# Feed-forward of a decoder layer in FP32 on TensorE: Strassen block products for two of eight K pairs, hidden rows turned through DRAM

## What is computed

```python
x = layer_norm(DEEPNORM_ALPHA * x + merged @ w_out[l], ln_g[l, 0], ln_b[l, 0])
ffn = (jax.nn.silu(x @ w_gate[l]) * (x @ w_up[l])) @ w_down[l]
x = layer_norm(DEEPNORM_ALPHA * x + ffn, ln_g[l, 1], ln_b[l, 1])
```

## Time and profile before

| | us |
|---|---|
| three runs | 1892.26, 1892.47, 1892.53 |
| median | 1892.47 |
| span of the profiled execution | 1889.9 |

### The profile page before, as it was taken

The page is one execution under the profiler, slowest core; times in us unless marked ns, Lnnn a source line. Parts: engine busy times, 40 slices in busy tenths (PEclk is TensorE's granted clock), DMA queues, the critical chain, the costliest instruction groups (busy, mean ns, idle before and its releaser), DMA issues.

```text
span 1889.9 us, 29981 instructions
## 1 busy us (share of the span) xinstructions
PE 1876.0 (99%) x9647; PEld 1548.7 (82%) x9647; DVE 1322.6 (70%) x1859; ACT 919.6 (49%) x1234; POOL 184.7 (10%) x448
## 2 busy tenths in 40 slices
PE   9999999999999999999999999999999999999997
PEld 7888888878888888888888887888888888888886
DVE  7878888888676767675677657577775466654656
ACT  5656565664455555556444447444443444443442
POOL 0202020020023233333000000000000000000000
PEclk9999999999999999999999999999999999999999
DMA  7667666575567776776665775566666666665565
GB/s 276 220 202 223 204 214 225 188 242 166 189 198 240 219 245 214 241 222 209 203 193 195 233 237 169 199 189 195 193 196 194 191 192 197 191 196 192 190 192 175
DMA packets 121041, 389.69 MB, mean 206 GB/s; under 512 B 14512, under 2 KB 27632, under 8 KB 120816
## 3 DMA queue, kind: packets, MB, share of 16 engines
q1 hardware_dynamic: 97904, 351.65, 58.2%
q10 hardware_dynamic: 19200, 28.34, 4.9%
q0 software_dynamic: 3840, 8.39, 1.6%
HBM read 368.91 MB, written 19.42 MB: 205 GB/s over the span
## 4 chain that ended last, share of the span: by engine, by line
PE 97%; DVE 1%; DMA 0%; issue 0%; ACT 0%; SPq 0%; DVEq 0%; ACTq 0%
PE pg L496 92%; PE B L496 5%; DVE gates L1474 1%; DMA raw<-in_weights 0%; PE B L596 0%; ACT whi L870 0%; PE B L816 0%; DVE wlo L1466 0%; DVE act_b L1466 0%; PE B L744 0%; DVE lnst L2170 0%; DVE sm L1474 0%; DVE act_a L1466 0%; DVE lnst L2175 0%; ACT L1390 0%
## 5 line engine op out<-in xcount | busy, mean ns | idle before, releaser
L1466 DVE TENSOR_TENSOR wlo<-raw,whi 128x1024 fp32r<-128x1024 f32 (+1 forms) x640 | 778.6, 1219 | 472.8 <-ACT whi L870 454.2
L870 ACT ACTIVATE whi<-raw 128x1024 fp32r<-128x1024 f32 (+1 forms) x640 | 674.3, 1057 | 751.8 <-PE pg L496 706.2
L496 PE MATMUL pg<-whi,act_x 128*128 128x512 f32 x2960 | 936.2, 393 | 1.0 <-ACT whi L870 1.0
L496 PEld LDWEIGHTS pg<-whi,act_x 128*128 128x128 f32 x2960 | 555.6, 188 | 120.2 <-issue 3.7
L496 PE MATMUL pg<-wlo,act_x 128*128 128x512 f32 x1480 | 574.7, 390 | 0.0
L496 PE MATMUL pg<-whi,act_a 128*128 128x512 f32 x1632 | 504.7, 389 | 0.1
L496 PEld LDWEIGHTS pg<-whi,act_a 128*128 128x128 f32 x1632 | 306.3, 188 | 64.2 <-DVE act_a L1466 0.8
L496 PEld LDWEIGHTS pg<-wlo,act_x 128*128 128x128 f32 x1480 | 278.1, 188 | 54.9
L496 PE MATMUL pg<-wlo,act_a 128*128 128x512 f32 x816 | 317.5, 389 | 0.0
L496 PEld LDWEIGHTS pg<-wlo,act_a 128*128 128x128 f32 x816 | 153.2, 188 | 31.7
L496 PE MATMUL pg<-whi,act_b 128*128 128x512 f32 x512 | 158.4, 389 | 0.0
(11 more groups left out here) (264 smaller groups left out, 1067.8 us busy)
## 6 DMA issues: line engine op xcount, KB each, us to landing
raw<-in_weights SPq DMA_DIRECT2D x646, 512.0 KB, 4.3
turn_c<-hraw ACTq DMA_DIRECT2D x8, 512.0 KB, 3.3
qT<-turn_c ACTq DMA_DIRECT2D x32, 128.0 KB, 4.5
turn_q<-hraw ACTq DMA_DIRECT2D x6, 512.0 KB, 4.5
gates<-turn_q ACTq DMA_DIRECT2D x24, 128.0 KB, 4.6
turn_p<-gates POOLq DMA_DIRECT2D x12, 192.0 KB, 3.4
gates<-turn_p POOLq DMA_DIRECT2D x48, 48.0 KB, 4.0
decm<-sums_out ACTq DMA_DIRECT2D x4, 512.0 KB, 3.9
```

The costliest lines, as they stand in the source:

```text
L496: return nc.tensor.matmul(o, l, r, start=start, stop=stop)
L870: return nc.scalar.activation(o, i, ACT.Copy, scale=scale)
L1466: return V.tensor_tensor(o, a, b, op)
```

## The change

Groups f = 1 to 10 take gate and up tiles in turn: tile 2p is rows of K pair p of the gate, tile 2p + 1 the same rows of the up matrix. For p in SPOS = (2, 5) the two tiles are one Strassen product (its form with seven products): two halves of the tokens by two K chunks by gate and up. The sums of weight blocks (v13, v24) are made by VectorE from raw and split into hi and lo like any weight (h13, l13, h24, l24); the sums of x are made once, at the end of group 0 (xs). The even tile then has four block products (12 TensorE products), the odd one three (9). They go into four banks of their own besides the four of gate and up rows, which they share partly; VectorE combines them at step 13 (shared_out), after tile 14 (gate_out) and at step 0 of the next group (up_out), and q1 is copied by ScalarE at step 12. silu now runs after gate_out, and the product with it at step 3 of the next group. pg and B take turns as the groups' own banks.

The product is written in another order of columns, goes to DRAM at step 5 and comes back at step 8 in four reads, and one transpose of 128x1024 at step 11 turns it; hi follows at step 12, lo at step 14. The gain goes to steps 5 and 10. All loops of the part are written out, and semaphores of the prologue are merged (not shown; its order of work is the same). The weights lie in memory as before; SyncE loads them in the new order.

```diff
-GAIN = (11, 13)
+GAIN = (5, 10)
+SPOS = (2, 5)
+NS = len(SPOS)
+H_AT, H_AWAY, H_BACK, H_TURN, H_HI, H_LO = 3, 5, 8, 11, 12, 14
...
+        def banks(f):
+            own, other = ([B[0:2], B[2:4]], pg[0] + pg[1])
+            if f in (2, 4, 5, 7, 10):
+                own, other = pg, B
+            return own, other
+        def down_bank(piece, i):
+            if piece == 0:
+                return B[2 * (i % 2):2 * (i % 2) + 2]
+            if piece == 1:
+                return pg[i % 2]
+            return [B[2:4], pg[1], pg[0], pg[1]][i]
+        def is_mixed(s):
+            return 0 <= s < 2 * TPG and s // 2 in SPOS
...
+            def later_in(n, s, at):
+                r = s % RING
+                sp.wait_ge(hi_done, n + s - RING + 1)
+                sp.wait_ge(lo_done, n + s - RING + 1)
+                sp.dma_start(raw[:, r].rearrange("p k n -> p (k n)"), weights[at]).then_inc(raw_full[r], 16)
+            def up(f):
+                for s in range(2 * TPG if f else 0):
+                    later_in(up_at(f), s, up_at(f) + s % 2 * TPG + s // 2)
+            def down(piece, n, f):
...
+            def product(bank, xh, xl, wh, wl, start, stop):
+                mm(bank[:, :], xh, wh, start, False)
+                mm(bank[:, :], xh, wl, False, False)
+                return mm(bank[:, :], xl, wh, False, stop)
+            def plain_tile(m, x, k0, own, first, last):
+                r = m % RING
+                pe.wait_ge(hi_done, m + 1)
+                pe.wait_ge(lo_done, m + 1)
+                for k in range(TK):
+                    for t in range(TOK):
+                        a = slice(t * P, (t + 1) * P)
+                        end = product(own[t], x[:, 0, k0 + k, a], x[:, 1, k0 + k, a], whi[:, r, k, :], wlo[:, r, k, :],
+                                      first and k == 0, last and k == TK - 1)
+                end.then_inc(tile_used, 1)
+            def mixed_tile(f, n, s):
+                own, other = banks(f)
+                v, i, k, m = mixed(f), SPOS.index(s // 2), s // 2 * TK, n + s
+                r, first, last = m % RING, i == 0, i == NS - 1
+                t0, t1 = slice(0, P), slice(P, SEQ)
+                pe.wait_ge(hi_done, m + 1)
+                pe.wait_ge(lo_done, m + 1)
+                if s % 2 == 0:
+                    product(other[0], act_a[:, 0, k, t0], act_a[:, 1, k, t0], whi[:, r, 0], wlo[:, r, 0], first, last)
+                    product(own[0][0], act_a[:, 0, k + 1, t0], act_a[:, 1, k + 1, t0], whi[:, r, 1], wlo[:, r, 1], False, False)
+                    product(other[3], xs[:, i, 2, 0], xs[:, i, 2, 1], v["h13"][:, 0], v["l13"][:, 0], first, last)
+                    end = product(other[2], xs[:, i, 1, 0], xs[:, i, 1, 1], v["h13"][:, 1], v["l13"][:, 1], first, last)
+                else:
+                    product(own[1][0], xs[:, i, 3, 0], xs[:, i, 3, 1], whi[:, r, 1], wlo[:, r, 1], False, False)
+                    product(other[1], xs[:, i, 0, 0], xs[:, i, 0, 1], v["h24"][:, 0], v["l24"][:, 0], first, last)
+                    end = product(own[0][1], act_a[:, 0, k + 1, t1], act_a[:, 1, k + 1, t1], v["h24"][:, 1], v["l24"][:, 1],
+                                  False, False)
+                end.then_inc(tile_used, 1)
...
+            def shared_ready(f):
+                if f in (1, 5, 9):
+                    for e in range(2):
+                        pe.wait_ge(evac[e], E0 + 1 + f // 4 * 2)
+                else:
+                    pe.wait_ge(gate_free, f - 1)
+                    pe.wait_ge(up_free, f - 1)
+                pe.wait_ge(xs_lo, 1)
...
+                tiles, buf = (TPG, TPG, LAST)[piece], (act_x, act_b, act_x)[piece]
+                pe.wait_ge(N["dve_mT"], 1 + NB + f)
                 for i in range(4):
-                    pe.wait_ge(evac[i % 2], g + i // 2)
+                    down_ready(piece, i)
+                    at = down_bank(piece, i)
...
+            def mixed_item(f, n, s):
+                m, v, i = n + s, mixed(f), nth(f, s)
+                r = m % RING
+                act.wait_ge(raw_full[r], 16 * (m // RING + 1))
+                act.wait_ge(tile_used, m - AHEAD)
+                if s % 2 == 0:
+                    copy(whi[:, r], raw[:, r]).then_inc(s_hi, 1)
+                    act.wait_ge(v_sum, 3 * i + 1)
+                    copy(v["h13"], v["v13"]).then_inc(hi_done, 1)
+                else:
+                    copy(whi[:, r, 1], raw[:, r, 1]).then_inc(s_hi, 1)
+                    act.wait_ge(v_sum, 3 * i + 3)
+                    copy(v["h24"], v["v24"]).then_inc(hi_done, 1)
+            def turn_h(f, s):
+                if s == H_AWAY:
+                    act.wait_ge(N["dve_m"], 1 + NB + f + 1)
+                    rows_away(flat(hraw[:, :, :]), turn_q, q_kept)
+                if s == H_BACK:
+                    act.wait_ge(q_kept, 16 * (HEADS_TURNED + f + 1))
+                    blocks_back(turn_q, landed(hraw), q_full)
+                if s == H_HI:
+                    act.wait_ge(N["dve_turn"], 1 + NB + f)
+                    copy(hi(*hidden(f), 4), turned).then_inc(N["act_mT"], 2)
+            def up(f):
+                n = up_at(f)
+                for s in range(0 if f else TPG - 1, 2 * TPG):
+                    if f and is_mixed(s + AHEAD):
+                        mixed_item(f, n, s + AHEAD)
+                    elif f or s > TPG:
                         split(n, s)
+                    if f not in (0, 5, 9):
+                        turn_h(f - 1, s)
+                    if f and s == S_END:
+                        act.wait_ge(tile_used, n + S_END)
+                        copy(mixed(f)["q1"], banks(f)[1][0][:, :]).then_inc(q1_done, 1)
+                    if f and s == 2 * TPG - 1:
+                        act.wait_ge(gate_free, f)
+                        nc.scalar.activation(vda[:, :, :], vda[:, :, :], ACT.Silu).then_inc(silu_done, 1)
...
+            def mixed_item(f, n, s):
+                m, v, i = n + s, mixed(f), nth(f, s)
+                r = m % RING
+                if s % 2 == 0:
+                    for e in range(2):
+                        dve.wait_ge(raw_full[r + e], 16 * (m // RING + 1))
+                    tt(v["v13"], raw[:, r:r + 2, 0], raw[:, r + 1, 0:2], ALU.add).then_inc(v_sum, 1)
+                    dve.wait_ge(s_hi, 2 * i + 1)
+                    dve.wait_ge(tile_used, m - AHEAD)
+                    tt(wlo[:, r], raw[:, r], whi[:, r], ALU.subtract)
+                    dve.wait_ge(v_sum, 3 * i + 1)
+                    tt(v["v24"][:, 0], v["v13"][:, 0], raw[:, r + 1, 1], ALU.add).then_inc(v_sum, 1)
+                    dve.wait_ge(v_sum, 3 * i + 2)
+                    tt(v["v24"][:, 1], v["v24"][:, 0], raw[:, r, 1], ALU.add).then_inc(v_sum, 1)
+                    dve.wait_ge(hi_done, m + 1)
+                    tt(v["l13"], v["v13"], v["h13"], ALU.subtract).then_inc(lo_done, 1)
+                else:
+                    dve.wait_ge(s_hi, 2 * i + 2)
+                    dve.wait_ge(tile_used, m - AHEAD)
+                    tt(wlo[:, r, 1], raw[:, r, 1], whi[:, r, 1], ALU.subtract)
+                    dve.wait_ge(hi_done, m + 1)
+                    tt(v["l24"], v["v24"], v["h24"], ALU.subtract).then_inc(lo_done, 1)
+            def shared_out(f):
+                v, other = mixed(f), [b[:, :] for b in banks(f)[1]]
+                dve.wait_ge(q1_done, f)
+                lnc(tt(v["w"][:, 0], v["q1"], other[1], ALU.add))
+                lnc(tt(v["u3"], v["w"][:, 0], other[2], ALU.add))
+                tt(v["w"][:, 0], other[3], v["w"][:, 0], ALU.subtract)
+                tt(v["w"][:, 1], other[3], v["u3"], ALU.subtract).then_inc(shared_free, 1)
+            def gate_out(f):
+                v, own = mixed(f), banks(f)[0]
+                dve.wait_ge(tile_used, up_at(f) + 2 * TPG - 1)
+                tt(vda[:, 0], own[0][0][:, :], v["q1"], ALU.add)
+                tt(vda[:, 1], own[0][1][:, :], v["u3"], ALU.add).then_inc(gate_free, 1)
+            def up_out(f):
+                v, own = mixed(f), banks(f)[0]
+                dve.wait_ge(tile_used, up_at(f) + 2 * TPG)
+                dve.wait_ge(shared_free, f)
+                for t in range(TOK):
+                    last = tt(v["w"][:, t], v["w"][:, t], own[1][t][:, :], ALU.add)
+                last.then_inc(up_free, 1)
+            by_channel = flat(hraw[:, :, :]).rearrange("p (b h t i) -> p t h b i", b=4, h=HB, t=TOK)
+            def by_head(ap):
+                return ap.rearrange("p (h b i) -> p h b i", h=HB, b=4)
+            def product(f):
+                dve.wait_ge(silu_done, f)
+                dve.wait_ge(up_free, f)
+                w = mixed(f)["w"]
+                if f == FG - 1:
+                    tt(hraw[:, :, :], w, vda[:, :, :], ALU.mult).then_inc(N["dve_m"], 1)
+                    return
+                for t in range(TOK):
+                    last = tt(by_channel[:, t], by_head(w[:, t]), by_head(vda[:, t]), ALU.mult)
+                last.then_inc(N["dve_m"], 1)
```

(108 more changed lines are left out.)

232 lines of the change are left out of this document (126 added, 106 removed).

## The result

The changed kernel takes 1895.17 us (median of 19 runs from 1890.7 to 1900.9; one more run, of 3817.8 us, is left out), the kernel before 1892.26 us (20 runs, 1891.2 to 1894.1). The ratio is 1.0016, interval 1.0009 to 1.0023: **slower by 3 us** where 5.6 us faster was forecast. The 60 products are gone and give 13.6 us, so something new costs 16.5 us. The profiled execution, one of the shorter ones, took 1892.59 us with a span of 1890.4.

What follows compares the result with a forecast made beforehand. TensorE's number of products was taken to bound the kernel. Saving 13.6 us and adding 8.0 us of waits gave -5.6 us, so 1886.9 us from the median 1892.47; range 1879 to 1899.

Steps and rivals of the forecast that it cites:

- 60 products, 13.6 us, in full unless TensorE waits: Two mixed pairs in each of ten groups save 60 TensorE products of 0.2267 us, 13.6 us off the end.
- Spacings 1.14, 0.605, 0.72, a sum of 38.3: VectorE's instructions overlap, so its queue in f = 2 to 4 sums to 38.3 us against TensorE's 42.16.
- The slower rival: Long mixed VectorE instructions don't overlap, so VectorE's queue is the bound: 19.4 us of waits, 1898.3 us; chance 0.22.
- 2.1 us behind silu, margin 0.5 at the first mixed tile, waits at f = 2, 3, 4, 7, 8: VectorE waits 2.1 us at group end, has 0.5 us margin, enters late: 5.8 us of TensorE waits at five entries.
- the down starts: Three down pieces begin with TensorE waiting for the lo of step 14: 0.5 us each, 1.5 us.
- 0.7 for landings: Term added for load landings to 7.3 us of TensorE waits, making 8.0 us.
- the turn adds 1 MB: Turn's traffic through DRAM on top of the group's 8.4 MB: DMA about 0.69 busy, counted as costing nothing.
- what costs nothing: List of added work taken as hidden: turn's traffic, its write and reads, sums of x, shared banks, written-out loops.
- the issues at 0.7 us a group: Four reads back from DRAM hold ScalarE's queue 1.92 us at step 8; about 0.7 reaches VectorE.
- the forecast's 1.35: On-time start of VectorE's split, 1.35 us after a tile's first product: 0.25 + 1.06 + 0.04.
- My second rival: Loads become late, two places in each of six turning groups: waits near 15, time 1894 us; chance 0.20.

Runs made afterwards that it cites:

- One pair: Changed kernel with only pair 5 mixed (SPOS = (5,)) in place of 2 and 5: 1886.24 us, ratio 0.9965.
- the last version: Changed kernel with silu behind the next split, pairs 3 and 5, wlo before v13, xs before ring buffers, transpose, hi, lo at steps 10, 11, 12: 1879.64 us.
- 11.3 (silu): Changed kernel with silu of the gate rows moved behind the next group's first split on ScalarE: 1883.83 us, ratio 0.9949.
- 8.3 us (GpSimd): Changed kernel with the ten turns through DRAM issued by GpSimd in place of ScalarE: 1886.86 us, ratio 0.9969.
- The single moves: Four edits, each alone on the changed kernel: silu later 1883.83 us, pairs 3 and 5 1886.84, turns issued by GpSimd 1886.86, wlo ahead of v13 1889.17.
- the pairs: Changed kernel with mixed pairs 3 and 5 in place of 2 and 5: 1886.84 us, ratio 0.9976.
- the gain: Changed kernel with the gain and bias of y moved from f = 1 to 4 into the first down piece: 1896.81 us, ratio 1.002.
- xs moved: Changed kernel with nothing but xs put ahead of the ring buffers in SBUF: 1895.12 us, ratio 1.0015.
- the kernel with unsummed x: Changed kernel with block products taking unsummed x in place of xs, output another: 1893.53 us in one run.
- the turn sooner: Three moves (silu later, pairs 3 and 5, wlo before v13) with xs moved, plus transpose, hi and lo at steps 10, 11, 12: 1879.64 us, ratio 0.9934.

## Why the prediction was wrong

- *60 products, 13.6 us, in full unless TensorE waits:* right. One pair gave 6.1 us with no wait, the last version 42.16 us a group.
- *Spacings 1.14, 0.605, 0.72, a sum of 38.3:* right, 38.9 busy at most. The slower rival as I put it, a VectorE without overlap, fell (its own terms add to 41.2, not 41.5), since the long mixed ones also start 1.14 us apart. I had read the Trainium skill (VectorE: DVE Perf Modes, "The DRAIN you can't avoid") in part only: behind the rule that the pipe must be empty first it says "A next op that is not held starts earlier", and the trace agrees with that, 1.14 us apart for 1.22 long.
- *2.1 us behind silu, margin 0.5 at the first mixed tile, waits at f = 2, 3, 4, 7, 8:* the places are right and 2.08 is measured. In the profiled execution the entries took 6.7 us for 5.8, the down starts 1.6 of idle for 1.5; together 8.3 for 8.0.
- **The step that failed** is "0.7 for landings", and with it "the turn adds 1 MB" under what costs nothing, and the issues at 0.7 us a group. Letting VectorE do one split ahead of the wait for rows gave back 6.0 us; leaving the turn's way out gave 12.2. Two things meet at step 7. The split that frees the slot is late, so the load is issued late (at f = 2 VectorE's split of tile 7 starts 3.8 us behind the first product of tile 4, where the forecast's 1.35 is on time); and the load goes out just behind the turn's write and takes 4.9 to 6.0 us, not 4.3. v13, which wants two tiles' rows, waits 1.5 to 2.6 us in seven groups, so VectorE wins back less of its lag. My second rival, loads late, with waits near 15 and 1894 us, had the landing (5.2, at most 6.1) and the place right, with a chance of 0.20. It expected two places a group; there is one, and it costs more.
- That the lag goes round a ring, VectorE, SyncE, DMA, VectorE, with ScalarE's issues in it, is my reading of these runs; no run follows one lag round. The waits for rows are not the loss by themselves: they rose to 18.1 and 18.5 us in the kernels that won 11.3 (silu) and 8.3 us (GpSimd). The single moves gave back 11.3, 8.3 (the pairs), 8.3 and 6.0 of the 16.5 us. They add to more than 16.5, so they take the same loss in part; and the gain, where VectorE then waits, gave nothing.
- *A wait costs its idle time, nothing for the clock and for the products' own rate:* the second miss. In the profiled execution it is nearly all of the miss, since 8.0 of its 8.3 us of idle were forecast. The clock cost 1.7 us, the products' rate 1.6, stopping and starting again 1.7, and 0.8 is not assigned. No row of before showed any of them; a range from both sides was due. That the idle came out near 8.0 is in part luck: it is one of the shorter executions, 2.6 us under the median.
- The range, 1879 to 1899, held the time. The time is 0.14% over the 1892.47 that the forecast started from, within its 0.2%, which had 0.23 against 0.52 for faster; it lies 1.2 us over the rival of late loads and 3.1 under that of a VectorE without overlap.

What stays open: how the 4 us between GpSimd's turns and no turns divide, what GpSimd's earlier issues did, what the 2.6 us between the profiled execution and the median are made of, and why the place of xs matters to TensorE.

## What to carry to other kernels

When an engine's queue, its waits included, comes within a few per cent of the bounding engine's, don't only add up its work; follow one lag round the ring of slots (split, slot free, load, next split) and ask whether it comes back smaller, and what other transfer starts beside that load. Price a wait of the bounding engine above its idle time: here 8.3 us of idle came with 3.4 us of clock and restarts. Look in each queue for an instruction that waits for a slower engine and stands ahead of one that others need: putting silu one place later was worth 11 us, while moving work between two steps that the same tile waits for was worth nothing. And if the bounding engine has begun to wait, a better rate of its own (xs moved) shows only after the waits are gone.

## What the hardware showed that was not expected

- Products whose held operand was xs, at the end of SBUF, and those around them followed each other by 0.232 us; with xs ahead of the ring buffers, or x itself held, by 0.2267.
- After an idle of 2.15 us TensorE's next products stood 0.43 us apart, and twelve took 4.41 us, before 0.23 came back (granted clock 0.83 over 10 us), while the clock stood at 1.00 around the idle of 2.12 us at f = 3. The same stretch of 0.43 stands behind idles of 2.04 and 2.35 us in the kernel with unsummed x and of 2.00 us in that with xs moved alone.
- The changed kernel's runs spread over 10.2 us, those of the kernel before over 2.8; the two kernels whose profile has no wait of TensorE in the part, one pair and the turn sooner, over 1.6 and 2.6 (five runs each).
- A load of 512 KB issued 0.4 to 1.2 us behind the turn's write took 4.9 to 6.0 us in seven places; without the turn 3.8 to 5.0 in the same places.
